# Spread stage of an expert-routing kernel: one-hot rows and gated columns formed token by token by VectorE in fp32, without bf16 masks and without ScalarE's cast

## The chip, the cores and the metric

The kernel runs on one core of one Trainium2 chip. The metric is the device time of one execution in microseconds. TensorE, VectorE, ScalarE and GpSimd run their own instruction streams; SyncE (SP in the profile) issues most of the transfers. Semaphores tie them together.

## What is computed

The kernel is one step of a one-layer streaming encoder: a combined projection, band attention and multi-scale retention, a merge, and then PEER, a layer that for each token picks 8 heads x 16 experts out of 128 x 128 single-neuron experts. The part that matters here is how the chosen experts and their gates are laid out for the expert layer. In the reference:

```python
top_s, top_i = lax.top_k(s, P_TOPK)
cand_s = (top_s[:, :, 0, :, None] + top_s[:, :, 1, None, :]).reshape(t, P_HEADS, P_TOPK * P_TOPK)
cand_i = (top_i[:, :, 0, :, None] * P_KEYS + top_i[:, :, 1, None, :]).reshape(t, P_HEADS, P_TOPK * P_TOPK)
best_s, best_pos = lax.top_k(cand_s, P_TOPK)
expert = jnp.take_along_axis(cand_i, best_pos, axis=-1)
gate = jax.nn.softmax(best_s, axis=-1)
a = jnp.einsum('td,thkd->thk', hb, expert_u[expert]).astype(jnp.float32)
act = (jax.nn.gelu(a, approximate=False) * gate).astype(hb.dtype)
return jnp.einsum('thk,thkd->td', act, expert_v[expert])
```

For 640 of the 1088 tokens (five tiles of 128) the kernel runs all experts densely and multiplies by a gate that is zero for experts that were not chosen. The spread stage makes that dense 128 x 128 gate array of every such token from its 128 choices. A choice has two places, i and j, and a gate value w; the array of a token is the sum over its choices s of onehot(i_s) times w_s onehot(j_s), a product of two 128 x 128 matrices with the choices on the contracted axis.

## The kernel before, in words

Stages follow one another, each closed by a barrier of all engines: projection (`project`), attention and retention (`mix`), routing (`route`), `spread`, `experts`. Routing ends with a store of the choices, turned so that a token is a column: `d["route"]` has 128 partitions (the choices) and three planes, place i, place j, and gate, of 640 tokens each. `spread` loads it as `rt`.

`spread` works in 80 steps of B = 8 tokens, 16 steps to a tile of 128 tokens, five tiles. In a step:

- VectorE makes three instructions of 128 x 1024 elements. L1618 compares a bf16 table that counts 0 to 127 for each token (`places_j`) with the bf16 places j of the eight tokens, broadcast along j, and gives the mask `hot_j`. L1622 does the same for place i with another table (`iotas`, tokens innermost) and gives `hot_i`. L1627 multiplies `hot_j` by the gates and gives `cols` in fp32.
- ScalarE turns `hot_i` around to token-major and casts it to fp32, `rows` (L1660), and, one step behind, copies the finished gates from PSUM to the tile's buffer (L1664).
- TensorE multiplies `rows` by `cols`, one 128 x 128 x 128 fp32 product for each token (L1643). The trace has two records for each.

Buffers: `rows` and `cols` have two slots, `gp` (PSUM) four banks, and the gate tile two slots, `spr_g` (g0, in the stage's own memory) and `pass_g` (o.g1, in memory that the expert stage takes over for its weights, gates and ring). The semaphores let VectorE write slot q % 2 of `cols` when the product of two steps ago is done (`spread_ready`), let ScalarE write `rows` under the same condition, and let TensorE write a PSUM bank when the copy of four steps ago is done (`g_out`). FREE = 2 and BANKS = 4 are the slots that are free at the start. In `rows_ready` the two free slots are counted in at the start, so that VectorE may write `hot_i` ahead of the cast.

SyncE stores a tile's gates (8 MB, L1582) when its last copy is done. Behind the fourth store it waits for it to land, then loads the first expert blocks (L1591, L1593), the residual rows (L1594) and the choices of the other tokens (L1529, L1532). The fifth tile is stored by the expert stage in four pieces (L1785). The first work of the expert stage is ScalarE's cast of a block of u (L1869), GpSimd's low part (L1809) and TensorE's products (L2077).

The loops of VectorE, TensorE, ScalarE and SyncE go over pairs of tiles with a hardware loop (`tiles`, L1562) and an odd tile behind it. Before the first step VectorE waits for an iota from GpSimd (L1601), makes the two tables (L1607, L1609), waits for `rt`, and makes the bf16 copy of the places (L1612).

## Time and profile before

| what | value |
|---|---|
| median of 3 runs | 3537.25 us (3533.98 to 3540.88) |
| the profiled execution's own time | 3545.49 us |
| its span in the profile | 3543.7 us |
| mean granted TensorE clock | 0.976 |
| the spread stage, from the first instruction of VectorE that uses `rt` to the end of the last copy | 1469.13 to 1715.77 us, 246.6 us |
| busy in the stage, per step | VectorE 3 instructions, ScalarE 2, TensorE 16 records |

The profile gives busy time by engine and by line, what ended the idle time before a group of instructions, the instructions in order of time, and DMA transfers. The duration of a VectorE instruction in the profile overlaps with the next one: the next starts before the row of the one before has ended. What an instruction costs a busy engine is therefore the distance between two starts, and it is shorter than the duration.

### The profile page before, as it was taken

The page shows a single profiled execution, that of the slowest core. Times are in us where ns is not written, and L with a number is a line of the kernel's source. Part 1 is how long each engine was busy: PE and PEld are TensorE (multiplying, and loading weights), DVE is VectorE, ACT ScalarE, POOL GpSimd, SP SyncE. Part 2 cuts the span into 40 slices and gives each one's busy share as a digit, 9 for nine tenths or more (in the row PEclk, how much of TensorE's full clock was granted, in tenths as well). Part 3 has the DMA queues.
Part 4 walks back from the last instruction along what each step waited for, and adds up shares of the span by engine and source line. Part 5 has one row for each costly group of instructions (what it writes and reads, how often), then busy time and mean ns, then how long its engine had stood idle before and what let it go on. Part 6 is the DMA issues. An engine that isn't in the chain of part 4 may idle for free.

```text
span 3543.7 us, 51514 instructions
## 1 busy us (share of the span) xinstructions
PE 3300.5 (93%) x18470; PEld 2844.1 (80%) x18470; DVE 2497.5 (70%) x5310; ACT 1079.8 (30%) x1689; POOL 1762.4 (50%) x1341
## 2 busy tenths in 40 slices
PE   8999996999997999367799999999999999999999
PEld 6888885556655999366689999998998899899898
DVE  3111103444331899899489999999999999999998
ACT  3222212343430222399522222222222222222221
POOL 0000004322220346200378888888878788888785
PEclk9999997999998999799999999999999999999999
DMA  4222215222214000065989999999999999999997
GB/s 176 101 92 101 94 63 209 76 103 87 96 63 149 21 19 18 17 174 160 309 330 368 379 370 368 380 369 350 382 362 361 362 373 368 376 375 368 360 372 285
DMA packets 338482, 831.47 MB, mean 235 GB/s; under 512 B 25904, under 2 KB 132784, under 8 KB 336048
## 3 DMA queue, kind: packets, MB, share of 16 engines
q0 software_dynamic: 129024, 469.82, 35.0%
q1 hardware_dynamic: 180752, 319.86, 25.7%
q10 hardware_dynamic: 28576, 40.31, 3.1%
q8 instruction: 51, 0.84, 0.1%
q14 instruction: 79, 0.65, 0.1%
HBM read 741.09 MB, written 88.80 MB: 234 GB/s over the span
## 4 chain that ended last, share of the span: by engine, by line
PE 46%; DVE 3%; DMA 1%; issue 1%; POOL 0%; SPq 0%; ACT 0%; DVEq 0%
PE exp_up L2077 23%; PE exp_vp L2094 23%; DVE exp_now L2024 1%; DMA scratch_gates<-spr_g 1%; DVE pass_g L2017 0%; DVE pass_g L1995 0%; DVE exp_ring L2017 0%; DMA pass_g<-in_u 0%; DVE exp_up L1981 0%; SPq L1785 0%; DVE exp_am_lo L1986 0%; DVE exp_now L2020 0%; POOL exp_v_lo L1814 0%; POOL exp_u_lo L1809 0%; POOL exp_ring L1823 0%
## 5 line engine op out<-in xcount | busy, mean ns | idle before, releaser
L2077 PE MATMUL exp_up<-dense_h_hi,exp_u_hi 128*128 128x320 f32 x2048 | 640.5, 313 | 23.5 <-POOL exp_u_lo L1809 14.0
L2077 PE MATMUL exp_up<-dense_h_lo,exp_u_hi 128*128 128x320 f32 x2048 | 634.5, 310 | 0.0
L2077 PE MATMUL exp_up<-dense_h_hi,exp_u_lo 128*128 128x320 f32 x2048 | 632.9, 309 | 0.0
L1995 DVE TENSOR_TENSOR pass_g<-pass_g,exp_vp 128x512 f32<-128x512 f32 x640 | 436.2, 682 | 110.1 <-PE exp_vp L2094 107.6
L2094 PE MATMUL exp_vp<-exp_v_hi,exp_am_hi 128*128 128x512 f32 x1280 | 504.5, 394 | 0.0
L2094 PE MATMUL exp_vp<-exp_v_hi,exp_am_lo 128*128 128x512 f32 x1280 | 503.4, 393 | 0.0
L2094 PE MATMUL exp_vp<-exp_v_lo,exp_am_hi 128*128 128x512 f32 x1280 | 501.9, 392 | 0.0
L1809 POOL TENSOR_TENSOR exp_u_lo<-pass_g,exp_u_hi 128x1024 fp32r<-128x1024 f32 x128 | 308.6, 2412 | 262.7 <-ACT exp_u_hi L1869 260.4
L2077 PEld LDWEIGHTS exp_up<-dense_h_hi,exp_u_hi 128*128 128x128 f32 x2048 | 386.4, 189 | 52.4 <-DVE exp_am_lo L1986 12.1
L2077 PEld LDWEIGHTS exp_up<-dense_h_lo,exp_u_hi 128*128 128x128 f32 x2048 | 385.7, 188 | 24.4
L2077 PEld LDWEIGHTS exp_up<-dense_h_hi,exp_u_lo 128*128 128x128 f32 x2048 | 386.3, 189 | 0.0
L1814 POOL TENSOR_TENSOR exp_v_lo<-pass_g,exp_v_hi 128x1024 fp32r<-128x1024 f32 x128 | 309.1, 2415 | 20.6 <-ACT exp_v_hi L1874 18.3
L1878 ACT ACTIVATE exp_up<-exp_up 128x320 f32<-128x320 f32 x256 | 108.0, 422 | 667.2 <-PE exp_up L2077 667.1
L340 PE MATMUL prj_zp<-prj_w_hi,prj_hT_hi 128*128 128x512 f32 x792 | 309.1, 390 | 0.0
L340 PE MATMUL prj_zp<-prj_w_lo,prj_hT_hi 128*128 128x512 f32 x792 | 308.6, 390 | 0.0
L1883 ACT CAST exp_am_hi<-exp_up 128x320 fp32r<-128x320 f32 x256 | 109.2, 426 | 650.4 <-DVE exp_up L1981 650.4
L2024 DVE SCALAR_TENSOR_TENSOR exp_now<-exp_ring,pass_g,exp_now 128x1024 f32<-128x1024 f32 x224 | 287.4, 1283 | 8.5
L2024 DVE SCALAR_TENSOR_TENSOR exp_now<-pass_g,exp_now 128x1024 f32<-128x1024 f32 x220 | 282.3, 1283 | 9.2 <-DVE exp_now L2024 0.9
L2094 PEld LDWEIGHTS exp_vp<-exp_v_lo,exp_am_hi 128*128 128x128 f32 x1280 | 241.2, 188 | 55.3
L340 PE MATMUL prj_zp<-prj_w_hi,prj_hT_lo 128*128 128x512 f32 x704 | 274.4, 390 | 0.0
L1455 PE MATMUL rt_qp<-rt_h2T,mid_late 128*128 128x128 f32 x2304 | 261.0, 276 | 9.4 <-DMA rt_h2T<-scratch_h2T 9.4
L2017 DVE CUSTOM_DVE_ANT_0 exp_ring<-exp_now,exp_ring 128x1024 f32<-128x1024 f32 x224 | 268.0, 1217 | 0.5 <-DMA exp_ring<-in_u_rows,pass_g 0.5
(216 smaller groups left out, 6073.1 us busy)
## 6 DMA issues: line engine op xcount, KB each, us to landing
pass_g<-in_u SPq DMA_DIRECT2D x126, 512.0 KB, 8.4
pass_g<-in_v SPq DMA_DIRECT2D x126, 512.0 KB, 6.5
pass_g<-scratch_gates SPq DMA_DIRECT2D x124, 320.0 KB, 6.6
scratch_z<-prj_zo ACTq DMA_DIRECT2D x33, 768.0 KB, 3.5
prj_w_raw<-in_w_in SPq DMA_DIRECT2D x44, 512.0 KB, 4.3
scratch_gates<-spr_g SPq DMA_DIRECT2D x2, 8192.0 KB, 30.4
scratch_gates<-pass_g SPq DMA_DIRECT2D x2, 8192.0 KB, 30.5
mix_zg<-scratch_z SPq DMA_DIRECT2D x9, 1024.0 KB, 5.3
```

Of the source, the lines that this page charges most:

```text
L340: last = nc.tensor.matmul(zp[:, bank(i), :], hT[p][:, k, i * P:(i + 1) * P], (w_hi, w_lo)[q][:, slot, k, :], start=(k == 0 and n == 0), st ...
L1455: last = nc.tensor.matmul(qp[:, hc % 3, 0:P], wq[:, k, hc * PK:(hc + 1) * PK], h2T[:, t % 2, k, :], start=(k == 0), stop=(k == KD - 1))
L1809: nc.gpsimd.tensor_tensor(u[1][:, j % 2, :], u_raw[:, j % 2, :], u[0][:, j % 2, :].bitcast(F32), ALU.subtract).then_inc(u_lo_ready, 1)
L1814: nc.gpsimd.tensor_tensor(v[j // 2 % 2][1][:, j % 2, :], v_raw[:, j % 2, :], v[j // 2 % 2][0][:, j % 2, :].bitcast(F32), ALU.subtract).the ...
L1878: nc.scalar.activation(up[:, g, 0:GW], up[:, g, 0:GW], ACT.Gelu).then_inc(gelu_ready, 1)
L1883: nc.scalar.copy(am[0][:, half, o, cols(g)], up[:, g, 0:GW]).then_inc(am_hi_ready, 1)
L1995: V.tensor_tensor(acc[:, t, c], acc[:, t, c], vp[:, n % 4, :], ALU.add).then_inc(added, 1)
L2017: V.tensor_tensor_reduce(out=row(n), in0=now[:, :], in1=row(n), scale=1.0, scalar=0.0, op0=ALU.mult, op1=ALU.add, accum_out=dot[:, c:c + 1 ...
L2024: V.scalar_tensor_tensor(out=now[:, :], in0=row(n), scalar=dot[:, c:c + 1], in1=now[:, :], op0=ALU.mult, op1=ALU.add).then_inc(taken, 1)
L2077: last = nc.tensor.matmul(up[:, g, 0:GW], u[a][:, o, k * P:(k + 1) * P], h2[b][:, k, cols(g)], start=(k == 0 and n == 0), stop=(k == KD - ...
L2094: last = nc.tensor.matmul(vp[:, bank, :], am[b][:, 1 - half, o, t * P:t * P + P], v[1 - half][a][:, o, c], start=(o == 0 and n == 0), stop ...
```

## The change

`rows` and `cols` are both written by VectorE, in fp32, by instructions that take one token each: `rows` of a token is a comparison of the iota with one value per partition, `cols` a comparison with one value per partition and a multiplication by another. A step is 8 instructions for `rows` and 8 for `cols`, each 128 x 128. The tables, the bf16 places, the two masks and ScalarE's cast are gone. Spare buffers of the same sizes keep all addresses. VectorE waits once a step, for `spread_ready`, ahead of `rows`; TensorE waits for `rows_ready` and `cols_ready` without the two counted in. VectorE's loop over tiles is written out (no hardware loop); those of TensorE, ScalarE and SyncE stay.

```diff
-        place = s.sb("place", [P, 2, NTD * P], BF16)
+        s.sb("spare2", [P, 2, NTD * P], BF16)
         iota = s.sb("iota", [P, P])
-        iotas = s.sb("iotas", [P, P, B], BF16)
-        hot_i = s.sb("hot_i", [P, 2, P, B], BF16)
-        places_j = s.sb("places_j", [P, B, P], BF16)
-        hot_j = s.sb("hot_j", [P, 2, B, P], BF16)
+        s.sb("spare", [P, 6 * B * P], BF16)
...
             dve.wait_ge(iota_set, 1)
-            nc.vector.tensor_copy(iotas[:, :, :], iota[:, :].rearrange("p (k o) -> p k o", o=1).broadcast_to([P, P, B])
-                                  ).then_inc(tables, 1)
-            nc.vector.tensor_copy(places_j[:, :, :], iota[:, :].rearrange("p (o k) -> p o k", o=1).broadcast_to([P, B, P])
-                                  ).then_inc(tables, 1)
             dve.wait_ge(rt_in, 16)
-            nc.vector.tensor_copy(place[:, :, :], rt[:, 0:2, :]).then_inc(tables, 1)
-            dve.wait_ge(tables, 3)
 
             def body(t, slot, pair, n):
                 for q, step in steps(t, n):
                     tok = t * P + q * B
-                    nc.vector.tensor_tensor(hot_j[:, q % 2, :, :], places_j[:, :, :],
-                                            place[:, 1, at(tok, B)].rearrange("p (b o) -> p b o", o=1).broadcast_to([P, B, P]),
-                                            ALU.is_equal).then_inc(hot_j_ready, 1)
-                    dve.wait_ge(rows_ready, step + 1)
-                    nc.vector.tensor_tensor(hot_i[:, q % 2, :, :], iotas[:, :, :],
-                                            place[:, 0, at(tok, B)].rearrange("p (o b) -> p o b", o=1).broadcast_to([P, P, B]),
-                                            ALU.is_equal).then_inc(hot_i_ready, 1)
-                    dve.wait_ge(hot_j_ready, step + 1)
                     dve.wait_ge(spread_ready, step + 1)
-                    nc.vector.tensor_tensor(cols[:, q % 2, :, :], hot_j[:, q % 2, :, :],
-                                            rt[:, 2, at(tok, B)].rearrange("p (b o) -> p b o", o=1).broadcast_to([P, B, P]),
-                                            ALU.mult).then_inc(cols_ready, 1)
-
-            tiles(dve, body)
+                    for b in range(B):
+                        last = nc.vector.tensor_scalar(rows[:, q % 2, b, :], iota[:, :], rt[:, 0, at(tok + b, 1)], None, ALU.is_equal)
+                    last.then_inc(rows_ready, 1)
+                    for b in range(B):
+                        last = nc.vector.tensor_scalar(cols[:, q % 2, b, :], iota[:, :], rt[:, 1, at(tok + b, 1)],
+                                                       rt[:, 2, at(tok + b, 1)], ALU.is_equal, ALU.mult)
+                    last.then_inc(cols_ready, 1)
+
+            for t in range(NTD):
+                body(t, t % 2, t // 2, P)
...
-                    pe.wait_ge(rows_ready, step + 1 + FREE)
+                    pe.wait_ge(rows_ready, step + 1)
...
-            act.sem_inc(rows_ready, FREE)
             act.sem_inc(g_out, BANKS)
...
-                def copy_rows(q, step):
-                    act.wait_ge(hot_i_ready, step + 1)
-                    act.wait_ge(spread_ready, step + 1)
-                    nc.scalar.copy(rows[:, q % 2, :, :], hot_i[:, q % 2, :, :].rearrange("p k b -> p b k")).then_inc(rows_ready, 1)
-
...
                 for q, step in steps(t, n):
-                    copy_rows(q, step)
-                    if q:
-                        gates_out(q - 1, step - 1)
-                gates_out(q, step)
+                    gates_out(q, step)
```

VectorE at the start of the spread stage, before: the tables, the loop's head, and the first step and a half (ISA rows are waits and register work).

```order
L1604 UNCONDITIONAL_BRANCH
L1607 CAST spr_iotas<-spr_iota 128x1024
L1609 CAST spr_places_j<-spr_iota 128x1024
L1612 CAST spr_place<-spr_rt 128x1280
L1564 UNCONDITIONAL_BRANCH
L1564 ISA
L1618 TENSOR_TENSOR spr_hot_j<-spr_places_j,spr_place 128x1024
L1621 ISA
L1622 ISA
L1622 TENSOR_TENSOR spr_hot_i<-spr_iotas,spr_place 128x1024
L1627 ISA
L1627 TENSOR_TENSOR spr_cols<-spr_hot_j,spr_rt 128x1024
```

The same place with the change, behind the last instructions of routing; the last two rows are one step, and they repeat 80 times with nothing between them.

```order
L1430 RECIPROCAL rt_den<-rt_den 128x4
L1433 TENSOR_TENSOR rt_out<-rt_shift,rt_den 64x4x16 x2
L80 UNCONDITIONAL_BRANCH
L1600 UNCONDITIONAL_BRANCH
L1610 TENSOR_SCALAR spr_rows<-spr_iota,spr_rt 128x128 x8
L1613 TENSOR_SCALAR spr_cols<-spr_iota,spr_rt 128x128 x8
```

Three wide instructions of a step have become sixteen narrow ones, and the three at the stage's start are gone.

ScalarE at the same place, before: two casts ahead of the first copy, then a cast and a copy in turn.

```order
L1649 UNCONDITIONAL_BRANCH
L1564 UNCONDITIONAL_BRANCH
L1564 ISA
L1658 ISA
L1660 CAST spr_rows<-spr_hot_i 128x1024
L1658 REGISTER_ALU
L1660 CAST spr_rows<-spr_hot_i 128x1024
L1663 REGISTER_ALU
L1664 COPY spr_g<-spr_gp 128x128x8
```

With the change only the copies are left:

```order
L1636 UNCONDITIONAL_BRANCH
L1560 UNCONDITIONAL_BRANCH
L1560 ISA
L1644 ISA
L1645 COPY spr_g<-spr_gp 128x128x8
L1644 REGISTER_ALU
L1645 COPY spr_g<-spr_gp 128x128x8
```

## Rows read from the trace of the kernel before

**Rows 1.** The page: span, and busy time of each engine over the span.

```profile
span 3543.7 us, 51514 instructions
PE 3300.5 (93%) x18470; PEld 2844.1 (80%) x18470; DVE 2497.5 (70%) x5310; ACT 1079.8 (30%) x1689; POOL 1762.4 (50%) x1341
```

**Rows 2.** Groups by line, 1440 to 1760 us: busy us, mean ns, idle before, releasers.

```profile
L1643 PE MATMUL spr_gp<-spr_cols,spr_rows 128*128 128x128 f32 x1280 | 170.6, 290 | 84.5 <-ACT spr_rows L1660 84.5
L1660 ACT CAST spr_rows<-spr_hot_i 128x1024 f32<-128x1024 bf16 x80 | 167.7, 2102 | 12.7 <-DVE spr_hot_i L1622 12.7
...
L1627 DVE TENSOR_TENSOR spr_cols<-spr_hot_j,spr_rt 128x1024 f32<-128x1024 bf16 x80 | 97.3, 1216 | 10.5 <-PE spr_gp L1643 10.5
L1618 DVE TENSOR_TENSOR spr_hot_j<-spr_places_j,spr_place 128x1024 bf16<-128x1024 bf16 x80 | 97.2, 1215 | 0.3 <-DVE spr_place L1612 0.3
L1622 DVE TENSOR_TENSOR spr_hot_i<-spr_iotas,spr_place 128x1024 bf16<-128x1024 bf16 x80 | 54.5, 681 | 0.0
```

**Rows 3.** Timeline, one step of the third tile: start us, us, engine, line.

```profile
1592.43 2.05 PE L1643 MATMUL spr_gp<-spr_cols,spr_rows 128*128 128x128 f32 x16 [0.81 <-ACT spr_rows L1660]
1592.53 1.22 DVE L1627 TENSOR_TENSOR spr_cols<-spr_hot_j,spr_rt 128x1024 f32<-128x1024 bf16 x1
1593.17 2.07 ACT L1660 CAST spr_rows<-spr_hot_i 128x1024 f32<-128x1024 bf16 x1
1593.67 1.21 DVE L1618 TENSOR_TENSOR spr_hot_j<-spr_places_j,spr_place 128x1024 bf16<-128x1024 bf16 x1
1594.80 0.68 DVE L1622 TENSOR_TENSOR spr_hot_i<-spr_iotas,spr_place 128x1024 bf16<-128x1024 bf16 x1
1595.12 1.02 ACT L1664 COPY spr_g<-spr_gp 128x1024 f32<-128x1024 f32 x1
...
1595.29 2.05 PE L1643 MATMUL spr_gp<-spr_cols,spr_rows 128*128 128x128 f32 x16 [0.80 <-ACT spr_rows L1660]
1595.40 1.22 DVE L1627 TENSOR_TENSOR spr_cols<-spr_hot_j,spr_rt 128x1024 f32<-128x1024 bf16 x1
```

**Rows 4.** Timeline, the stage's start and its end.

```profile
1469.13 0.83 DVE L1612 CAST spr_place<-spr_rt 128x1280 bf16<-128x1280 f32 x1 [3.26 <-DMA spr_rt<-scratch_route]
...
1712.67 2.05 PE L1643 MATMUL spr_gp<-spr_cols,spr_rows 128*128 128x128 f32 x16 [0.79 <-ACT spr_rows L1660]
1714.76 1.01 ACT L1664 COPY spr_g<-spr_gp 128x1024 f32<-128x1024 f32 x1 [1.23 <-PE spr_gp L1643]
...
1716.68 1.99 ACT L1869 CAST exp_u_hi<-pass_g 128x1024 fp32r<-128x1024 f32 x2 [0.91 <-PEq L82]
```

**Rows 5.** Timeline of VectorE in routing: narrow single-source instructions back to back.

```profile
1426.17 0.22 DVE L1357 TENSOR_SCALAR rt_part<-rt_bi 128x128 uint32<-128x128 uint32 x1
1426.30 0.22 DVE L1358 TENSOR_SCALAR rt_part<-rt_bi 128x128 uint32<-128x128 uint32 x1
1426.44 0.26 DVE L1359 CAST rt_place<-rt_bi 128x128 bf16<-128x128 uint32 x1
```

**Rows 6.** Timeline of VectorE in the projection: without, then with a per-partition scalar.

```profile
22.99 2.36 DVE L280 TENSOR_TENSOR prj_w_lo<-prj_w_raw,prj_w_hi 128x1024 fp32r<-128x1024 f32 x2 [0.25 <-ACT prj_w_hi L204]
...
31.41 3.68 DVE L265 SCALAR_TENSOR_TENSOR prj_h<-front_early,prj_rs,prj_gain 128x1024 f32<-128x1024 f32 x3 [0.97 <-POOL prj_rs L177]
```

**Rows 7.** Groups of VectorE by line, whole span: per-partition scalar, then constants.

```profile
L2024 DVE SCALAR_TENSOR_TENSOR exp_now<-exp_ring,pass_g,exp_now 128x1024 f32<-128x1024 f32 x224 | 287.4, 1283 | 8.5
...
L280 DVE TENSOR_TENSOR prj_w_lo<-prj_w_raw,prj_w_hi 128x1024 fp32r<-128x1024 f32 x44 | 52.0, 1221 | 230.9 <-ACT prj_w_hi L204 230.9
...
L265 DVE SCALAR_TENSOR_TENSOR prj_h<-front_early,prj_rs,prj_gain 128x1024 f32<-128x1024 f32 x9 | 11.2, 1281 | 4.0 <-POOL prj_rs L177 4.0
...
L1399 DVE SCALAR_TENSOR_TENSOR rt_eid<-rt_out 128x128 uint32<-128x128 f32 x4 | 1.1, 272 | 0.0
```

**Rows 8.** Transfers, 1455 to 1800 us: KB each, median us to landing.

```profile
scratch_gates<-pass_g SPq DMA_DIRECT2D x2, 8192.0 KB, 30.5
...
pass_g<-in_u SPq DMA_DIRECT2D x6, 512.0 KB, 5.9
```

**Rows 9.** Timeline of SyncE's queue: the fourth store, and the first load behind it.

```profile
1667.21 0.37 SPq L1582 DMA_DIRECT2D scratch_gates<-pass_g  x1
1697.86 0.84 SPq L1591 DMA_DIRECT2D pass_g<-in_u  x2
```

**Rows 10.** Windows, PE alone: us, busy us (records), granted clock, DMA share, GB/s.

```profile
1571.00:1575.00 4.00, 3.68 (x17) 0.50 1.02 291
...
1592.00:1595.00 3.00, 2.05 (x16) 1.00 1.02 290
```

More of the change, by code:

```diff
@@ L1552, in spread @@
         gp = s.pb("gp", [P, BANKS, B * P])
-        rt_in, iota_set, tables = s.sem("rt_in"), s.sem("iota_set"), s.sem("tables")
-        hot_i_ready, hot_j_ready = s.sem("hot_i_ready"), s.sem("hot_j_ready")
+        rt_in, iota_set = s.sem("rt_in"), s.sem("iota_set")
         rows_ready, cols_ready = s.sem("rows_ready"), s.sem("cols_ready")
```

## The prediction

> **What bounds the kernel now.** I begin with the page. It shows a span of 3543.7 us with TensorE busy in 93% of it, VectorE in 70%, ScalarE in 30% [rows 1]. These are averages over stages. The change touches one stage alone, so the second view is the groups by line in that stretch. TensorE's products there were busy for 170.6 us, and in front of them it stood idle for 84.5 us, all of it put down to ScalarE's cast [rows 2]. So TensorE is not the bound here. The cast took 2102 ns a piece, and the three instructions of VectorE 1216, 1215 and 681 ns [rows 2]. Read as durations both engines have more than 3.1 us of work in a step.
>
> The third view, the timeline of one step, tells what a step takes. TensorE's groups start at 1592.43 and 1595.29, a step of 2.86 us [rows 3]. VectorE starts L1627 at 1592.53, L1618 at 1593.67, L1622 at 1594.80 and the next L1627 at 1595.40: 1.14 + 1.13 + 0.60 = 2.87 us, no gap. ScalarE is full too: from the cast's start at 1593.17 to the copy's at 1595.12 are 1.95 us, and the rest of the 2.86 us, 0.91, is the copy. **Two engines bound the step together**, at the same 2.87 us. A lighter ScalarE alone would bring nothing; what the change is worth is what VectorE's share of a step becomes. TensorE's sixteen records take 2.05 us on the clock from first start to last end [rows 3], and it can begin the next step somewhat before that end.
>
> The stage runs from 1469.13, when `rt` has landed and VectorE first uses it, to 1714.76 + 1.01 = 1715.77, when the last copy ends. The expert stage begins 0.9 us later with ScalarE's cast of u [rows 4]. A later end of this stage delays everything behind it by the same amount: the barrier holds all engines, and the blocks of u were in by then.
>
> 80 steps of 2.87 us are 229.6 us. The other 17 us are the start (bf16 places, the first step) and the tile boundaries, where cast and copies come in another order.
>
> **The change, part by part.** *Removed from ScalarE:* 80 casts. It keeps 80 copies of 0.91 to 1.02 us [rows 3], far under a step. It no longer bounds anything. At a tile boundary nothing of it is in VectorE's way any more.
>
> *Removed from VectorE:* the three wide instructions of a step, 2.87 us, and in front of the first step the bf16 places (0.83 us, [rows 4]). The two tables were made while `rt` was on its way, so they bring nothing. The first row is formed at about 1469.1.
>
> *Added to VectorE:* 16 instructions of 128 x 128 fp32 a step, 1280 in all. The trace has no such instruction with a per-partition scalar, so the price is put together from two rows. The base is L1357 and L1358: one source of 4-byte elements in SBUF, 128 x 128, with constants. They start at 1426.17, 1426.30 and, the one behind, 1426.44: 0.135 us from start to start [rows 5]. 128 elements in that time are already faster than one element a cycle: VectorE's 128x1024 fp32 instructions that go back to back, L280, take 2.36 - 1.22 = 1.14 us from start to start for eight times the width [rows 6, 7], which is 1.07 us for 1024 elements if what is fixed is 0.07 us. By that the narrow one spends 0.067 us on its elements (two a cycle) and 0.068 us on being an instruction.
>
> The second part is the scalar read from memory. L265 has one, `rs`. Three of them take 3.68 us, so (3.68 - 1.28) / 2 = 1.20 us from start to start, against 1.14 us for L280, which has none [rows 6]. By durations it is 1281 and 1283 ns against 1221 ns [rows 7]. That it is the scalar and not the form of the instruction is shown by L1399: the same form with a constant took 272 ns for 128 elements, 133 ns of elements and 139 ns of the rest, while 1283 - 1067 leaves 216 ns. So a scalar from memory costs 0.060 to 0.077 us; I take 0.065. The new instruction: **0.135 + 0.065 = 0.200 us**, a step 16 x 0.200 = 3.20 us, against 2.87 before.
>
> Bounds of this price: below, 0.135 us, if at this width the scalar is read beside other work; above, for `cols`, which reads two scalars, 0.265 us, if each is paid; and for all sixteen 0.267 us, if the instruction runs at one element a cycle (0.133 + 0.068 + 0.065). I take 0.200 since the rows with a scalar show the full surcharge at back-to-back starts, and the nearest row to the two reads of one instruction is none.
>
> The Trainium skill has a rule for this, "VectorE: DVE Perf Modes", section "The TRN2 errata": an SBUF-to-SBUF instruction costs 58 cycles plus its elements over the mode's factor, at 0.96 GHz. For 128 elements two a cycle that is an estimate of 127 ns, with no term for a scalar from memory; by it a step would be 2.03 us. The same section says that many small tiles pay the fixed part again and again and advises 512 elements and more, which speaks against this change. The trace agrees with the fixed part (0.068 us), and shows a surcharge that the rule lacks.
>
> *TensorE* waits for `rows` and `cols` of a step instead of for the cast. A product of 8 tokens takes 2.05 us, less than 3.20, so it follows VectorE. VectorE's one wait, for the product of two steps ago, has 3.20 - 2.05 = 1.1 us to spare; behind it the sixteen instructions are queued, and they do not wait. TensorE's wait for a free bank and ScalarE's for the store (30.5 us, [rows 8], against a tile of 51 us) have been met long before. The hardware loop's turn falls away on VectorE and stays on the others, where 1.1 us of slack a step takes it in.
>
> *SyncE:* the same transfers behind the same events. The loads of u and v are issued when the fourth store has landed, 30.6 us after its issue [rows 9], and had 18 us before the stage ended; a fifth tile of 51 us gives them 20.
>
> **The sum.** Start 1469.1, plus 80 x 3.20 = 256.0, plus the tail: TensorE's last product, from its start at 1712.67 to the copy's at 1714.76, 2.09 us, the copy 1.01 us [rows 4], and 0.1 us of hand-over, 3.2 us. The stage ends at 1728.3 in place of 1715.8: **+12.5 us**. The profiled execution (3545.49 us) would become 3558.0. It was 8.2 us over the median of the runs shown, so the median goes from 3537.25 to 3549.8 us. A measurement of this kernel tells about 0.2%, 7 us, from no change.
>
> **The rivals.**
>
> *A, the forecast:* one scalar or two, 0.065 us. +12.5 us, 3549.8. A price of 0.195 to 0.205 us gives 3543 to 3556.
>
> *B, each scalar is paid.* `cols` costs 0.265 us: a step 8 x 0.200 + 8 x 0.265 = 3.72 us, 297.6 us for the stage, +54 us, 3591. For it: the only rows with a scalar have one, and show that it is not hidden. Against: two reads in a row of one instruction could share one latency.
>
> *C, faster: the scalar costs nothing at this width.* The surcharge is seen only on instructions of 1024 elements with two sources; if it grows with the elements (0.06 us in 1.07) it is 0.008 us here. Then a step is 16 x 0.135 = 2.16 us, still above TensorE, 172.8 us in all; the stage ends at 1645.1, 70.7 us earlier. Part goes back: the fourth store would be issued at about 1610.5 and land at 1641.0, the loads of u need 5.9 us more [rows 8], and the fifth store and the picks queue close behind; I take 7 us. -64 us, 3474. The point from which it decides: below 0.179 us an instruction the step is shorter than 2.87 us, below about 0.190 us the kernel is faster. The skill's rule above is this case, at a step of 2.03 us. Against it: L1399 and L2024 differ by 77 ns in what is fixed.
>
> *D, one element a cycle.* If comparing with a scalar from memory keeps VectorE from taking two elements a cycle, a step is 16 x 0.267 = 4.27 us, 341.6 us, +98 us, 3635. For it: no row shows two a cycle together with a scalar from memory. Against: uint32 with constants shows it [rows 5], and the engine has one source here.
>
> *E, TensorE's clock.* With 1.1 us of idle time in every step the granted clock may stay at its lower level (0.50 of 2.4 GHz, as for 3.68 us behind the idle time at a tile boundary, where 17 records took those 3.68 us, [rows 10]). Sixteen records then take 3.46 us, more than 3.20, and TensorE bounds: 276.8 us, +33 us, 3571. Against: at 0.8 us of idle time a step the clock was 1.00 [rows 10].
>
> **How the numbers follow.** Chances: A 0.42, B 0.23, C 0.15, D 0.15, E 0.05. The likeliest is A, 3549.8 us. The range leaves out C: from 3542, the lower side of A, to 3640, the upper side of D; it holds about 0.84. Faster by over 0.2%: C and a little of A, 0.17. Within 0.2% (to 3544.3): the lower edge of A, 0.06. Slower: 0.77.
>
> **What would show it.** In the changed profile, L1610 and L1613 at about 285 ns of duration (219 + 65), starts 0.200 us apart, a step of 3.20 us; the last copy at about 1727; TensorE idle in front of its products for VectorE's `cols`, not for ScalarE, some 1.1 us a step; ScalarE idle for TensorE. If L1613 starts 0.265 us apart it is B, if L1610 does too, D, with durations near 350 ns; if starts are 0.135 us apart, C, and then the expert stage's first cast waits for a DMA. A granted clock of 0.5 in the middle of the stage would be E. I am wrong altogether if VectorE shows idle time within its sixteen instructions.

## The result, and the profile after

The changed kernel takes 3585.92 us (median of 4 runs, 3582.65 to 3589.34) against 3537.21 us for the kernel before (4 runs): ratio 1.0134, interval 1.0121 to 1.0146. It is slower by 48.7 us, not by the 12.5 us of the forecast. The profiled execution took 3588.43 us, 2.5 us over its median, with a span of 3586.6 us.

The page's first lines, after (compare [rows 1]):

```profile
span 3586.6 us, 52035 instructions
PE 3293.1 (92%) x18470; PEld 2839.2 (79%) x18470; DVE 2555.2 (71%) x6347; ACT 931.1 (26%) x1609; POOL 1762.4 (49%) x1341
```

The groups of the stage (1440 to 1800 us), after: busy us, mean ns, idle time before, releasers. They answer to [rows 2].

```profile
L1613 DVE TENSOR_SCALAR spr_cols<-spr_iota,spr_rt 128x128 f32<-128x128 f32 x640 | 181.6, 476 | 0.0
L1630 PE MATMUL spr_gp<-spr_cols,spr_rows 128*128 128x128 f32 x1280 | 164.3, 282 | 138.3 <-issue 124.0 <-DVE spr_cols L1613 14.3
...
L1610 DVE TENSOR_SCALAR spr_rows<-spr_iota,spr_rt 128x128 f32<-128x128 f32 x640 | 142.8, 414 | 11.7 <-DMA spr_rt<-scratch_route 11.4 <-PE spr_gp L1630 0.3
L1645 ACT COPY spr_g<-spr_gp 128x1024 f32<-128x1024 f32 x48 | 48.6, 1012 | 138.6 <-PE spr_gp L1630 138.6
L1645 ACT COPY pass_g<-spr_gp 128x1024 f32<-128x1024 f32 x32 | 32.4, 1012 | 83.4 <-PE spr_gp L1630 83.4
```

VectorE has one wait of size, 11.4 us for `rt` to land in front of the stage, and 0.3 us for TensorE. ScalarE, which bounded the stage before together with VectorE, now waits 222.0 us for TensorE (138.6 + 83.4), and TensorE stands idle for 138.3 us in place of 84.5; each of these sums has some 10 us in it that lie before the stage's first instruction. The rows put 14.3 us of TensorE's idle time to `cols`, which is the one wait in front of the first product, and the other 124.0 us to "issue", 1.6 us in each later step. The timeline shows what these are. One step of the changed kernel in the timeline, start and duration:

```profile
1585.43 1.76 DVE L1610 TENSOR_SCALAR spr_rows<-spr_iota,spr_rt 128x128 f32<-128x128 f32 x8
...
1585.72 2.02 PE L1630 MATMUL spr_gp<-spr_cols,spr_rows 128*128 128x128 f32 x16 [1.59 <-issue]
1587.00 2.24 DVE L1613 TENSOR_SCALAR spr_cols<-spr_iota,spr_rt 128x128 f32<-128x128 f32 x8
1587.78 1.01 ACT L1645 COPY pass_g<-spr_gp 128x1024 f32<-128x1024 f32 x1 [2.60 <-PE spr_gp L1630]
1589.05 1.76 DVE L1610 TENSOR_SCALAR spr_rows<-spr_iota,spr_rt 128x128 f32<-128x128 f32 x8
...
1589.34 2.02 PE L1630 MATMUL spr_gp<-spr_cols,spr_rows 128*128 128x128 f32 x16 [1.59 <-issue]
```

Eight `rows` go from 1585.43 to 1587.00: 1.57 us, 0.196 us each. Eight `cols` go from 1587.00 to 1589.05: 2.05 us, **0.256 us each**. The step is 3.62 us where the forecast had 3.20 and the kernel before 2.87 [rows 3]. TensorE's next products start at 1589.34, when the eighth `cols` has been formed (1587.00 + 2.24 = 1589.24), and 3.62 us after the last ones did. So the "issue" time is a wait for `cols`.

The stage's start and end, after, answering to [rows 4]:

```profile
1469.35 1.66 DVE L1610 TENSOR_SCALAR spr_rows<-spr_iota,spr_rt 128x128 f32<-128x128 f32 x8 [11.44 <-DMA spr_rt<-scratch_route]
...
1756.96 2.40 DVE L1613 TENSOR_SCALAR spr_cols<-spr_iota,spr_rt 128x128 f32<-128x128 f32 x8
...
1759.46 2.02 PE L1630 MATMUL spr_gp<-spr_cols,spr_rows 128*128 128x128 f32 x16 [1.59 <-issue]
1761.52 1.01 ACT L1645 COPY spr_g<-spr_gp 128x1024 f32<-128x1024 f32 x1 [2.60 <-PE spr_gp L1630]
...
1763.41 1.99 ACT L1847 CAST exp_u_hi<-pass_g 128x1024 fp32r<-128x1024 f32 x2 [0.88 <-PEq L82]
```

The last copy ends at 1762.53 in place of 1715.77, **46.8 us later**, and the expert stage's first cast follows 0.88 us after it, as before. From there to the end of the span are 1823.2 us after and 1827.0 us before, 3.8 us less. In the profiles of the twelve kernels below, which leave the expert stage as it is, the same part takes between 1822.4 and 1849.0 us, so 3.8 us are within what it varies by; why it varies was not traced. The stage's +46.8 us thus gives a span of +42.9 us here, while the medians differ by 48.7 us.

TensorE's clock in the stage, after (us, busy us and records of PE, PEld, VectorE, ScalarE and GpSimd, granted clock, DMA share, GB/s), answering to [rows 10]:

```profile
1475.00:1760.00 285.00, 160.98 (x1262) 148.27 (x1262) 284.08 (x1255) 79.96 (x79) 0.00 (x0) 0.99 0.47 137
```

VectorE is busy for 284.08 of 285 us. The granted clock was 0.99 of 2.4 GHz with 1.6 us of idle time in each step.

### The profile page after: what moved, and what is told of

Same layout as the page of the kernel before. It is cut to its first block, busy times and chain, and to the rows that moved or that the text cites. A ratio compares the mean times of both kernels' runs of the same rounds, so it can differ in the third digit from the quotient of the medians.

```text
span 3586.6 us, 52035 instructions
## 1 busy us (share of the span) xinstructions
PE 3293.1 (92%) x18470; PEld 2839.2 (79%) x18470; DVE 2555.2 (71%) x6347; ACT 931.1 (26%) x1609; POOL 1762.4 (49%) x1341
## 4 chain that ended last, share of the span: by engine, by line
PE 46%; DVE 2%; DMA 1%; POOL 1%; issue 1%; SPq 0%; ACT 0%; DVEq 0%
PE exp_up L2055 23%; PE exp_vp L2072 23%; DVE exp_now L2002 1%; DMA scratch_gates<-spr_g 1%; DVE pass_g L1995 0%; DVE pass_g L1973 0%; DVE exp_ring L1995 0%; POOL exp_v_lo L1792 0%; POOL exp_u_lo L1787 0%; POOL exp_ring L1801 0%; DVE exp_up L1959 0%; DMA pass_g<-in_u 0%; SPq L1763 0%; DVE exp_now L1998 0%; DVE exp_am_lo L1964 0%
## 5 line engine op out<-in xcount | busy, mean ns | idle before, releaser
L1630 PE MATMUL spr_gp<-spr_cols,spr_rows 128*128 128x128 f32 x1280 | 164.3, 282 | 138.3 <-issue 124.0
L1630 PEld LDWEIGHTS spr_gp<-spr_cols,spr_rows 128*128 128x128 f32 x1280 | 151.4, 194 | 151.4 <-issue 151.3
```

What stands on the lines that cost most here:

```text
L1630: last = nc.tensor.matmul(gp[:, q % BANKS, b * P:(b + 1) * P], rows[:, q % 2, b, :], cols[:, q % 2, b, :], start=True, stop=True)
```

## The experiments

Each compares with runs of the kernel before on the same chip; the medians of those were 3553.67 us (constants, one scalar, columns alone), 3543.19 (the changed kernel again, half width, rows alone, tokens innermost), 3552.41 (the next four) and 3562.44 (the last), so ratios and differences are compared, not times. "Start to start" is read from the timeline. Each experiment has a label (e1, e3 and so on), by which the expectations name one another.

### What a scalar costs: none, one, two

*No scalar from memory (e1).* The compared places and the gate are constants, so what is computed isn't the gates.

```
-  tensor_scalar(rows[...], iota[:, :], rt[:, 0, at(tok + b, 1)], None, ALU.is_equal)
+  tensor_scalar(rows[...], iota[:, :], 5.0, None, ALU.is_equal)
-  tensor_scalar(cols[...], iota[:, :], rt[:, 1, at(tok + b, 1)], rt[:, 2, at(tok + b, 1)], ...)
+  tensor_scalar(cols[...], iota[:, :], 7.0, 0.5, ...)
```

> Both scalars of both instructions are constants in place of values read from memory (the gates are then wrong numbers; count and width of the instructions stay). Theory 1 (two elements a cycle, and 0.06 us for each scalar read from memory): starts 0.135 us apart on both lines, a step of 2.16 us, the stage 116 us shorter than the changed kernel's, some 7 us given back at the start of the expert stage, 3473 to 3480 us. Theory 2 (one element a cycle, 0.133 + 0.065 = 0.198 us, the first scalar free and something else in cols worth 0.06 us): starts stay at 0.196 us in rows, cols 0.196 or 0.256 us, 3548 to 3586 us.

Measured: 3492.41 us, ratio 0.9828 [0.9811, 0.9844], 61 us under the kernel before. Its timeline, VectorE:

```profile
1589.82 1.18 DVE L1610 TENSOR_SCALAR spr_rows<-spr_iota 128x128 f32<-128x128 f32 x8
...
1590.90 1.17 DVE L1613 TENSOR_SCALAR spr_cols<-spr_iota 128x128 f32<-128x128 f32 x8
...
1591.99 1.17 DVE L1610 TENSOR_SCALAR spr_rows<-spr_iota 128x128 f32<-128x128 f32 x8
```

Both kinds take 0.135 us, which is the base of the forecast [rows 5]. The second operation, the product with 0.5, costs nothing. What follows: all that lies above 0.135 us in the changed kernel comes from the scalars. The step here was 2.21 us (22 steps from 1589.82 to 1638.43) and not 16 x 0.135 = 2.16: `rows` starts within 0.01 us of ScalarE's copy of a finished product (L1644 has starts at 1589.82 and 1591.99 too), which points at TensorE. VectorE hardly bounds this kernel any more.

*One scalar (e3).* `cols` reads its place but is scaled by 0.5 in place of the gate.

```
-  tensor_scalar(cols[...], iota[:, :], rt[:, 1, at(tok + b, 1)], rt[:, 2, at(tok + b, 1)], ...)
+  tensor_scalar(cols[...], iota[:, :], rt[:, 1, at(tok + b, 1)], 0.5, ...)
```

> Only the gate in cols is a constant 0.5 (the gates lose their values); the place is still read from memory. If the second scalar is what costs cols its 0.06 us: both lines 0.196 us apart, a step of 3.14 us, 3548 us. If it is the second operation (the multiplication): cols stays at 0.256 us, 3586 us.

Measured: 3557.1 us, ratio 1.0015 [1.0005, 1.0024]. VectorE's timeline:

```profile
1590.82 1.65 DVE L1610 TENSOR_SCALAR spr_rows<-spr_iota,spr_rt 128x128 f32<-128x128 f32 x8
...
1592.39 1.65 DVE L1613 TENSOR_SCALAR spr_cols<-spr_iota,spr_rt 128x128 f32<-128x128 f32 x8
...
1593.96 1.65 DVE L1610 TENSOR_SCALAR spr_rows<-spr_iota,spr_rt 128x128 f32<-128x128 f32 x8
```

1.57 us for eight of either kind, 0.196 us each, a step of 3.14 us. The one edit, the gate as a constant, takes the kernel from +1.3% to +0.15%: **the second scalar read is nearly all of the loss**. `cols` still has both operations here, so it is the read and not the multiplication. The series is 0.135, 0.196, 0.256 us: 0.061 us for the first, 0.060 us for the second.

*The changed kernel again, and with half the width (e5).* The second forms 64 of each 128 elements; the other halves hold zeroes, so the gates of those places are left out.

```
-  tensor_scalar(rows[:, q % 2, b, :], iota[:, :], rt[...], None, ALU.is_equal)
+  tensor_scalar(rows[:, q % 2, b, 0:P // 2], iota[:, 0:P // 2], rt[...], None, ALU.is_equal)
   (cols likewise)
```

> The changed kernel unaltered, beside the others of this group, as their reference: 1.4% over the kernel before, a step of 3.62 us. Its VectorE durations grow over the stage from 0.28 to 0.55 us (rows) while the starts stay 0.196 us apart. If that is a matter of the two scalars reading at this rate, it shows again; if it was that execution's alone, durations stay near 0.28 and 0.34 us.

> The changed kernel with instructions of 64 of the 128 elements, the other halves set to zero once before the stage's data arrive (half of the one-hot work is left out). Two elements a cycle: 0.033 us less each, starts 0.163 and 0.223 us apart, a step of 3.09 us, 42 us below the changed kernel. One element a cycle: 0.067 us less each, a step of 2.55 us, 85 us below. All of the price per instruction: no difference.

Measured: the changed kernel again 3588.65 us, ratio 1.0128 [1.0111, 1.0145]. Half width 3542.31 us, ratio 1.0007 [0.9996, 1.0018]; its VectorE:

```profile
1591.91 1.86 DVE L1615 TENSOR_SCALAR spr_cols<-spr_iota,spr_rt 128x64 f32<-128x64 f32 x8
...
1593.70 1.38 DVE L1612 TENSOR_SCALAR spr_rows<-spr_iota,spr_rt 128x64 f32<-128x64 f32 x8
...
1595.00 1.86 DVE L1615 TENSOR_SCALAR spr_cols<-spr_iota,spr_rt 128x64 f32<-128x64 f32 x8
```

1.79 / 8 = 0.223 us for `cols`, 1.30 / 8 = 0.163 for `rows`. Half the elements save 0.033 us on each, 0.52 ns an element, which is half the 1.04 ns (1.07 us for 1024) of the two-source fp32 instructions [rows 6]. So the instruction takes its elements at double that rate with one scalar and with two; rival D is out. Of 0.256 us only 0.067 are elements; 0.068 are the instruction and 0.121 its scalars.

### Each half of the change alone

*Columns direct, rows by mask and cast as before (e4):*

```
-  tensor_tensor(hot_j[...], places_j[...], place[:, 1, ...], ALU.is_equal)
   tensor_tensor(hot_i[...], iotas[...], place[:, 0, ...], ALU.is_equal)
-  tensor_tensor(cols[...], hot_j[...], rt[:, 2, ...], ALU.mult)
+  for b in range(B):
+      tensor_scalar(cols[:, q % 2, b, :], iota[:, :], rt[:, 1, at(tok + b, 1)], rt[:, 2, at(tok + b, 1)], ...)
```

> Half of the change: cols token by token as in the changed kernel (two instructions of 1.13 and 1.14 us give way to eight of 0.256 us), rows by the bf16 mask and ScalarE's cast as before. VectorE's step falls from 2.87 to 0.60 + 2.05 = 2.65 us, but ScalarE still needs 2.86 us: if the two engines bounded the step together, a step stays at 2.86 us and the kernel within 0.2% of before (3530 to 3540 us). If VectorE alone was the bound, a step of 2.65 us and 3520 us.

Measured: 3550.36 us, ratio 0.9986 [0.9976, 0.9995]: 2 to 9 us gained. The timeline of VectorE, ScalarE and TensorE:

```profile
1592.08 2.14 DVE L1624 TENSOR_SCALAR spr_cols<-spr_iota,spr_rt 128x128 f32<-128x128 f32 x8
...
1592.86 2.05 PE L1641 MATMUL spr_gp<-spr_cols,spr_rows 128*128 128x128 f32 x16 [0.82 <-ACT spr_rows L1658]
1593.59 2.07 ACT L1658 CAST spr_rows<-spr_hot_i 128x1024 f32<-128x1024 bf16 x1
1594.14 0.68 DVE L1619 TENSOR_TENSOR spr_hot_i<-spr_iotas,spr_place 128x1024 bf16<-128x1024 bf16 x1
1594.95 2.14 DVE L1624 TENSOR_SCALAR spr_cols<-spr_iota,spr_rt 128x128 f32<-128x128 f32 x8
```

VectorE now needs 8 x 0.256 + 0.60 = 2.65 us, 0.22 less than before, and stands in front of each L1624 (it starts 0.81 us after L1619, which takes 0.60). The step stays at 2.86 us (2.87 from these rows): cast and copy, 1.95 + 0.91 us as in [rows 3], fill ScalarE. In the profiled execution the stage took 245.6 us (1465.29 to 1710.91) against 246.6; where the rest of the few microseconds comes from is not shown. Of the statement that two engines bound the step together this tests one half, that a lighter VectorE alone brings nothing, and it holds; e10 below has the other.

*Rows direct, columns by mask and product as before (e6):*

```
-  for b in range(B):
-      tensor_scalar(cols[:, q % 2, b, :], iota[:, :], rt[:, 1, ...], rt[:, 2, ...], ...)
+  tensor_tensor(hot_j[...], places_j[...], place[:, 1, ...], ALU.is_equal)
+  tensor_tensor(cols[...], hot_j[...], rt[:, 2, ...], ALU.mult)
```

(a difference to the changed kernel; `rows` is formed between the two)

> The other half of the change: rows token by token on VectorE (8 x 0.196 = 1.57 us in place of 0.60 us and ScalarE's cast), cols by the mask and the multiplication as before (1.13 + 1.14 us). If VectorE's starts simply add, a step is 3.84 us and the kernel about 64 us above before, more than the whole change costs. If freeing ScalarE is worth something by itself, it lies below that.

Measured: 3605.57 us, ratio 1.0175 [1.0158, 1.0191], +62 us. VectorE's timeline:

```profile
1591.38 1.21 DVE L1614 TENSOR_TENSOR spr_hot_j<-spr_places_j,spr_place 128x1024 bf16<-128x1024 bf16 x1
...
1592.51 1.64 DVE L1619 TENSOR_SCALAR spr_rows<-spr_iota,spr_rt 128x128 f32<-128x128 f32 x8
...
1594.08 1.21 DVE L1622 TENSOR_TENSOR spr_cols<-spr_hot_j,spr_rt 128x1024 f32<-128x1024 bf16 x1
1595.21 1.21 DVE L1614 TENSOR_TENSOR spr_hot_j<-spr_places_j,spr_place 128x1024 bf16<-128x1024 bf16 x1
```

1.13 + 1.57 + 1.13 = 3.83 us. The direct rows cost VectorE 1.57 us where the mask with tokens innermost cost 0.60: **+0.97 us a step for the rows, -0.22 for the columns**. The rows' half moves a cast off ScalarE that VectorE pays for; the columns' half is a small gain for VectorE that ScalarE hides as long as the cast is there. In the whole change it counts, since the cast is gone: 0.97 - 0.22 = +0.75 us.

### Making the cast cheap instead

ScalarE's cast reads `hot_i` with tokens innermost and writes with places innermost. If everything has tokens innermost, it is a plain copy, and TensorE reads every eighth element (e7).

```
-  rows = s.sb("rows", [P, 2, B, P])
+  rows = s.sb("rows", [P, 2, P, B])        (cols and hot_j likewise)
-  nc.tensor.matmul(gp[...], rows[:, q % 2, b, :], cols[:, q % 2, b, :], ...)
+  nc.tensor.matmul(gp[...], rows[:, q % 2, :, b], cols[:, q % 2, :, b], ...)
-  nc.scalar.copy(rows[...], hot_i[:, q % 2, :, :].rearrange("p k b -> p b k"))
+  nc.scalar.copy(rows[...], hot_i[:, q % 2, :, :])
```

> The kernel before with tokens innermost in both masks and both fp32 buffers. VectorE: 0.60 + 0.60 + 1.14 = 2.34 us a step; ScalarE's cast no longer turns its input around and should fall from 1.95 to about 0.95 us; TensorE reads both operands every eighth element. If TensorE keeps its 2.05 us, the step is 2.34 us and the kernel 42 to 50 us below before. If TensorE's read of every eighth element is slower than 2.3 us for eight tokens, the gain shrinks, and from 2.9 us on it is a loss.

Measured: 3616.42 us, ratio 1.0205 [1.0188, 1.0222]. The cast did fall, from 2.10 to 1.05 us (mean durations), but TensorE became the bound. Two more kernels separate the operands: the first (e8) has only `rows` (which the weight loads read) with tokens innermost and `cols` formed directly; the second (e9) has only `cols` and its mask `hot_j` that way, the rest as before.

> As e4 (cols token by token, rows by mask and cast), but rows is kept with tokens innermost, so the cast reads and writes in order (0.95 us in e7) and TensorE loads its weights every eighth element. If the slow TensorE of e7 (3.9 us for eight tokens) came from the moving operand, TensorE keeps 2.05 us, VectorE bounds with 0.60 + 2.05 = 2.65 us, and the kernel lies 17 to 30 us below before. If it came from the weights, a step of about 3.9 us, 70 us above.

> The counterpart: the kernel before with cols alone tokens innermost, so that TensorE's moving operand is read every eighth element, and the mask of j costs VectorE 0.60 in place of 1.13 us. If the moving operand is the slow one, TensorE's step is 3.9 us and the kernel 70 us above before. If not, ScalarE's 2.86 us bounds as before: within 0.2% of before.

Measured: 3620.02 us, ratio 1.0189 [1.0171, 1.0206], and 3621.86 us, 1.0195 [1.0178, 1.0213]. TensorE's groups (1480 to 1760 us) with both strided:

```profile
L1641 PE MATMUL spr_gp<-spr_cols,spr_rows 128*128 128x128 f32 x1128 | 271.8, 421 | 8.7 <-ACT spr_rows L1658 8.7
```

with `rows` alone strided:

```profile
L1641 PE MATMUL spr_gp<-spr_cols,spr_rows 128*128 128x128 f32 x1137 | 272.0, 405 | 8.7 <-DVE spr_cols L1624 6.7 <-ACT spr_rows L1658 2.0
L1641 PEld LDWEIGHTS spr_gp<-spr_cols,spr_rows 128*128 128x128 f32 x1136 | 271.0, 335 | 9.4 <-DVE spr_cols L1624 7.2 <-ACT spr_rows L1658 2.2
```

and with `cols` alone strided:

```profile
L1641 PE MATMUL spr_gp<-spr_cols,spr_rows 128*128 128x128 f32 x1142 | 267.8, 413 | 12.6 <-ACT spr_rows L1658 12.6
L1641 PEld LDWEIGHTS spr_gp<-spr_cols,spr_rows 128*128 128x128 f32 x1141 | 239.1, 215 | 40.9 <-issue 10.8 <-ACT spr_rows L1658 3.4
```

TensorE is busy all the time at about 3.8 us for 8 tokens, in place of 2.05. Either operand read at every eighth fp32 element is enough: strided weights show in the loads (335 ns against 215), a strided moving operand in the products alone. Both together cost hardly more than one. The clock is not the cause: from 1480 to 1700 us it was 0.97, 0.97 and 0.96 of 2.4 GHz in the three, and 0.97 in the kernel before. So the transposing cast is what buys TensorE its 2.05 us.

### Sharing the work out otherwise

*One row of eight direct, columns direct; ScalarE casts seven (e10):*

```
+  CAST = 7
   tensor_tensor(hot_i[:, q % 2, :, 0:CAST], iotas[:, :, 0:CAST], place[:, 0, at(tok, CAST)], ...)
+  for b in range(CAST, B):
+      tensor_scalar(rows[:, q % 2, b, :], iota[:, :], rt[:, 0, at(tok + b, 1)], ...)
   (cols direct, as above; the cast takes 0:CAST)
```

> e4 with the eighth token's row formed by VectorE directly. ScalarE casts seven tokens: 0.91 + 7 x 0.244 = 2.62 us; VectorE 0.53 + 0.20 + 2.05 = 2.78 us. If both bound together, the step falls from 2.86 to 2.78 us: 6 us below e4, 8 to 10 us below before.

Measured: 3548.75 us, ratio 0.9991 [0.9978, 1.0004], no difference that can be told. The timeline of VectorE and ScalarE:

```profile
1592.55 2.13 DVE L1628 TENSOR_SCALAR spr_cols<-spr_iota,spr_rt 128x128 f32<-128x128 f32 x8
...
1594.60 0.73 DVE L1620 TENSOR_TENSOR spr_hot_i<-spr_iotas,spr_place 128x896 bf16<-128x896 bf16 x1
...
1595.22 0.26 DVE L1625 TENSOR_SCALAR spr_rows<-spr_iota,spr_rt 128x128 f32<-128x128 f32 x1
1595.36 1.84 ACT L1663 CAST spr_rows<-spr_hot_i 128x896 f32<-128x896 bf16 x1
```

2.05 + 0.62 + 0.19 = 2.86 us: VectorE bounds again, at the same step. ScalarE's cast starts at 1595.36, as the mask ends (1594.60 + 0.73 = 1595.33), so now ScalarE waits for VectorE. That is the other half of "two engines bound the step": ScalarE was relieved of an eighth of its cast, VectorE stayed full, and the step stayed. The mask of seven tokens took 0.62 us, not less than the 0.60 of eight, while the mask of six in the next kernel takes 0.47 (1594.58 to 1595.05). So seven is out of line, not narrow masks as such; whether that is because it is odd is open, since no other odd width was run. With the 0.53 us of a mask in proportion the step would have been 2.77 us.

*The product with the gate on GpSimd, two rows of eight direct (e11):*

```
+  pool: nc.gpsimd.tensor_tensor(cols[...], hot_j[...], rt[:, 2, ...], ALU.mult)
   dve:  hot_j mask; hot_i mask of 6 tokens; 2 x tensor_scalar(rows[...])
```

> Three engines share a step: VectorE both masks (1.13 us, and 0.47 us for six tokens) and two rows directly (0.39 us), 2.0 us; ScalarE casts six tokens and copies the gates, 0.91 + 6 x 0.244 = 2.37 us; GpSimd, idle so far, multiplies the mask by the gates, 2.41 us by its 128x1024 rows in the expert stage. If they do not disturb each other: a step of 2.41 us, 37 us below before, 85 us below the changed kernel. If GpSimd and VectorE hold each other up while both read, GpSimd's instruction takes over 2.9 us, and nothing is gained.

Measured: 3597.38 us, ratio 1.0128 [1.0111, 1.0146], +45 us. The timeline of VectorE and GpSimd (POOL):

```profile
1594.58 0.55 DVE L1633 TENSOR_TENSOR spr_hot_i<-spr_iotas,spr_place 128x768 bf16<-128x768 bf16 x1
1594.74 2.15 POOL L1610 TENSOR_TENSOR spr_cols<-spr_hot_j,spr_rt 128x1024 f32<-128x1024 bf16 x1 [1.49 <-DVE spr_hot_j L1629]
1595.05 2.11 DVE L1638 TENSOR_SCALAR spr_rows<-spr_iota,spr_rt 128x128 f32<-128x128 f32 x2
...
1597.08 1.21 DVE L1629 TENSOR_TENSOR spr_hot_j<-spr_places_j,spr_place 128x1024 bf16<-128x1024 bf16 x1
```

Two instructions that take 0.39 us in the changed kernel stand for 2.03 us, until GpSimd's has ended at 1596.89. To see which of VectorE's instructions are held up, the next kernel (e12) has none with a scalar: rows come in fp32 from one two-source comparison, without a cast, and GpSimd makes the product.

```
-  tensor_tensor(hot_i[...], iotas[...], place[:, 0, ...], ALU.is_equal)   and ScalarE's cast
+  tensor_tensor(rows[:, q % 2, :, :], places_j[:, :, :], place[:, 0, ...], ALU.is_equal)
```

> As e11, but no instruction of VectorE in the stage has one source alone: rows is written in fp32 by one comparison of two tensors, 128x1024 (1.13 us from start to start, as the mask of j), and ScalarE casts nothing. VectorE 1.13 + 1.13 = 2.27 us, GpSimd 2.15 us, TensorE 2.05 us, ScalarE 0.91 us. In e11 VectorE's masks (two sources) ran at full speed beside GpSimd's multiplication, and its single-source instructions stood until it ended. If that is what decides: a step of 2.27 us; the stage 60 us shorter than before, less up to 9 us given back at the start of the expert stage (e1): 50 to 60 us below before. If two-source instructions are held up too: a step of 1.13 + 2.15 + 1.13 = 4.4 us, over 100 us above.

Measured: 3639.1 us, ratio 1.0212 [1.0198, 1.0226], a step of 3.97 us. The same timeline of this kernel:

```profile
1594.61 1.21 DVE L1629 TENSOR_TENSOR spr_rows<-spr_places_j,spr_place 128x1024 f32<-128x1024 bf16 x1
1594.76 2.81 POOL L1608 TENSOR_TENSOR spr_cols<-spr_hot_j,spr_rt 128x1024 f32<-128x1024 bf16 x1 [1.16 <-DVE spr_hot_j L1625]
1595.74 2.91 DVE L1625 TENSOR_TENSOR spr_hot_j<-spr_places_j,spr_place 128x1024 bf16<-128x1024 bf16 x1
...
1598.58 1.21 DVE L1629 TENSOR_TENSOR spr_rows<-spr_places_j,spr_place 128x1024 f32<-128x1024 bf16 x1
```

A two-source instruction was held up here, while L1633 of the kernel before this one was not. Read in order of starts, both kernels say the same: whichever of the two engines begins first runs to its end, and the other stands. In this kernel GpSimd starts behind L1629 and, taken from that one's end at 1595.74 to its own end at 1597.57, needs 1.83 us; L1625, which began at 1595.74, then has 1.08 us left. In the one before, GpSimd starts behind L1633 and, from 1595.05 to 1596.89, needs 1.84 us. The expectation had read the first of these traces wrongly: by this order L1633 ran at full speed because it came first, not because it has two sources. That two independent reckonings give 1.83 and 1.84 us speaks for the new reading, but it rests on these two traces; GpSimd's instruction was not run with VectorE idle. By it, adding GpSimd to a full VectorE adds its time to the step: 1.13 + 0.47 + 1.84 + 0.2 = 3.64 us (measured 3.63), and 1.13 + 1.83 + 1.08 = 4.04 (3.97).

No version that computes the gates gains more than 0.3% over the kernel before. The columns alone are the one whose interval lies below 1: 0.9986, 2 to 9 us.

## Why the prediction was right and wrong, point by point

**The bound (right).** Both engines at 2.87 us. Relieving VectorE by 0.22 us left the step at 2.86 us, relieving ScalarE by an eighth of its cast did too, and with the cast gone the step was VectorE's.

**Right:** the base of 0.135 us (0.135 measured without scalars); the single scalar, 0.065 us (0.061; `rows` 0.196 against 0.200); elements at double the rate of the two-source instructions (0.52 against 1.04 ns); TensorE following with its 2.05 us (2.02), its clock at 0.99; ScalarE bounding nothing; the tail of 3.2 us (3.5, from 1756.96 + 8 x 0.256 to 1762.53); the place of the loads of u. The timeline of SyncE's queue, after:

```profile
1736.95 0.84 SPq L1587 DMA_DIRECT2D pass_g<-in_u  x2
```

26 us ahead of the stage's end, against 18 before [rows 9], so nothing waited for them. The form of the sum held too. Put into it, the step of the one-scalar kernel, 80 x 3.134 us, gives +12.5 - 5.3 = +7.2 us; its stage took 8.2 us more than before (1464.58 to 1719.46), and its ratio gives 5 us, between 2 and 9.

**The range held by its width.** 3585.92 us lies inside 3542 to 3640, but the range had been drawn from A to D, so that it took in B's time as well. The value called likeliest, +12.5 us, was a quarter of what came, and that the time fell inside is no merit of its sum.

**The step that failed** is "one scalar or two, 0.065 us". The instruction was priced at 0.200 us for `cols` too, with the reason that no nearby row had two reads. It measured 0.256 us: every scalar is paid. 8 x 0.056 us more a step, less 8 x 0.004 for `rows`, is 0.42 us, times 80 steps 33 us: of the 34.3 us between the forecast's +12.5 and the stage's +46.8, that is all but 1 us. The mechanism and the sign stood; one term was sized by the lower of its two bounds, though the text itself had the upper, and the only evidence on a scalar said it was not hidden. Rival B had the mechanism (0.265 us, +54 us) and came 5 us from the medians.

**Where the time went.** 80 steps of 3.616 us are 289.3 us against 229.6 us, +59.7. Against that stands what the forecast counted as removed: the first steps and tile boundaries. Before, the stage took 246.6 us, 17.0 more than its steps; after, 1469.35 to 1762.53 are 293.2 us, 3.9 more, nearly all of it the tail. So 13 us of boundaries and start went away (with the start 0.2 us later: 59.7 - 13.1 + 0.2 = 46.8). VectorE went through the boundaries at an even step since it waited for nobody. A change can remove every stall of a stage and lose by what it puts in their place.

**Rival C** came out near its price, 61 us gained for 64 given, but not by its terms. The stage took 181.4 us (1464.61 to 1646.03), 65.2 less than before and not 70.7, since TensorE held the step at 2.21 us. The give-back of 7 us was 9, and by another mechanism. Stage and give-back alone make 56 us; where the medians' other 5 come from is not traced. In the kernel with constants the expert stage's first cast waited 9.93 us, and the timeline of SyncE's queue and ScalarE shows for what:

```profile
1641.82 1.74 SPq L1587 DMA_DIRECT2D pass_g<-in_u  x2
...
1649.91 4.94 SPq L1532 DMA_DIRECT2D pass_g<-scratch_gate  x2
...
1655.96 1.99 ACT L1846 CAST exp_u_hi<-pass_g 128x1024 fp32r<-128x1024 f32 x2 [9.93 <-PEq L82]
```

The loads of u were issued at 1641.82 and the last copy of the stage ended at 1646.03, but the queue went on issuing until 1654.85, and the next stage's first cast and SyncE's next issue (1655.94) start together behind it: so it was 13 us of issuing that the barrier waited for, not the 5.9 us of data. In the changed kernel this lies in front of the end and costs nothing.

**The sign.** Without scalars the trace agrees with the Trainium skill, "VectorE: DVE Perf Modes", section "The TRN2 errata": 0.135 us measured, an estimate of 127 ns by its formula. Taken by itself it would have called this change a gain of some 60 us. The runs show what stands beside it here, 0.061 us for each scalar from memory, and that decided the sign: -1.7% with none, +0.15% with the one in each instruction, +1.3% with both in `cols`.

**Durations.** I said about 285 ns for both; they were 414 and 476 ns on average in the profiled execution. They are no measure here: those of `rows` grew from 281 ns to 547 ns in the course of the stage, while starts stayed 0.196 us apart. In the profile of the same kernel run again (e5) they were flat, 267 to 289 ns. Its VectorE groups:

```profile
L1613 DVE TENSOR_SCALAR spr_cols<-spr_iota,spr_rt 128x128 f32<-128x128 f32 x640 | 170.0, 330 | 0.0
...
L1610 DVE TENSOR_SCALAR spr_rows<-spr_iota,spr_rt 128x128 f32<-128x128 f32 x640 | 131.4, 270 | 12.3 <-DMA spr_rt<-scratch_route 12.1 <-PE spr_gp L1630 0.3
```

270 ns against 414 at the same time for the kernel (1.0128 and 1.0134). Steps were read right in the prediction because they were read from starts.

## What to carry to other kernels

Price a narrow instruction from start to start and count its operands one by one: here elements were a quarter of its cost and the two scalars nearly half, and where no row shows two of a kind, the honest default is that each is paid. Where two engines are level, moving work from one to the other loses unless it gets cheaper on the way: the row mask cost VectorE 0.60 us with its tokens innermost and 1.57 us token by token, and no gain on ScalarE could come back. And look at what a layout is for before undoing it, since the costly transposing cast was what kept TensorE at 2.05 us.

## What the runs showed of the hardware that I had not expected

- A scalar read from memory adds 0.061 us to a 128x128 fp32 instruction of VectorE, and a second one 0.060 us more: the second costs as much as the first. With 64 elements the second again adds 0.061 us (1.79 us against 1.30 for eight instructions); what the first adds was not measured there.
- TensorE reading either operand at every eighth fp32 element (32 bytes apart) takes about 3.8 us for 8 tokens in place of 2.05; ScalarE's cast takes 2.10 us when it transposes and 1.05 us when it doesn't (durations). The Trainium skill, "SBUF — State Buffer", section "Door 1: The DMA port swizzle", says that successive accesses that leave a 16-byte line pay a penalty; the runs agree with its direction and give it this size.
- VectorE and GpSimd wait for each other by whole instructions: 0.39 us of VectorE became 2.03. The Trainium skill, "SBUF — State Buffer", section "Who interferes with whom", has the rule (an exclusive hold of the shared pair by the one that starts first, for the whole instruction, with two-source and two-port instructions of VectorE alike), and both traces agree with it, though GpSimd's 1.84 us was not measured alone.
- A profile's durations of narrow instructions can double within one stage with unchanged starts (`rows` 0.281 to 0.547 us, starts 0.196 us apart).
